# Hybrid decoder step on one core: where the state-space output is turned, activated and split, and where the first GLU weights and x are loaded

## The chip, the cores and the metric

The kernel runs on one core of one Trainium2 chip. A core has TensorE (PE: matrix products and transposes), VectorE (DVE), ScalarE (ACT), GpSimd (POOL) and the engine that issues most DMA transfers, SyncE (SP). Each engine works through its own list in order and waits on semaphores. The metric is the time of one launch in microseconds (us), the median of several runs.

## The reference

One layer of a hybrid decoder for 256 prompt tokens and 8 samples of 8 tokens (320 columns in all), width 2048, all in f32:

```python
h = x * (1 + sc1) + sh1
q, k, v, u, ga, gb = split(h @ w_in)
att = stick_breaking(q, k_all, v_all)          # samples also read 1024 cached keys and values
y_s = s5(u, ssm_h0, ...)                       # state space branch, 1024 wide, plus d_skip * u
y_s = gelu(y_s)
y_s = y_s * sigmoid(y_s @ w_glu + b_glu)       # GLU, w_glu is 1024 x 1024
merged = sigmoid(ga) * (att @ w_att_br) + sigmoid(gb) * (y_s @ w_ssm_br)
x = layernorm(ALPHA * x + (1 + g1) * (merged @ w_out))
# then conv FFN, second layernorm
```

## The kernel before

Activations stand transposed: 128 features on the partitions, the 320 tokens in the free dimension, one such tile per block of 128 features (`KA` = 8 blocks for 1024 features, `KD` = 16 for 2048). Every f32 product is made of three products of rounded values: a value is split into a high part (`wH`, `ygH`, ... : rounded) and a low part (`wL`, `ygL`, ... : the rest), and `product` (L936 to L951) gives, for each of K blocks, high x high, high x low and low x high. For GLU and merge that is 8 blocks, 24 matmuls of 128x320 for each tile of the output. ACT makes the high part of a block of weights (L1251), DVE the low part (L1523), both one product ahead with two buffers, and SP loads weight blocks into a ring of four buffers (`load`, L440 to L443), each when the block four places before has been split. Semaphores `hi_done`, `split_done` and `chunk_done` count the blocks over the whole program in the order GLU (8), merge (32), out and so on.

The stages that matter here, in order of time:

1. Attention. `attend(i)` exists on every engine and is run for i = 0 to 8. It holds the front half for sample i (keys of 8 pages are loaded into `kpage`, transposed on PE as `flip`, copied by DVE and ACT, multiplied with the queries as `score`) and the back half for sample j = i - 1 together with prompt head j. The back half is a chain: `turn_scores` and `head_scores` on PE, `scores` and `head_scores` on DVE, `softplus` on ACT (Exp, then Ln) and DVE, `sums` on PE (with running sums over pages by POOL, `sR`), `log_weights` on DVE, `weights` on ACT (Exp), `outputs` on PE (values of 8 pages, L1117 to L1129), `copy_outputs` on ACT, `turn_outputs` on PE (L1142), `sample_output` on DVE. i = 1 to 7 are a loop; the last, `attend(SB, front=False)`, is written out and has a back half alone.
2. The state-space output. It was stored earlier by token in `y_tok`, and SP loads it back into `ytk` after attend(1) (L574, L575), with x behind it (L576, 2560 KB into `xT`, which had been spilled to `x_d`). After the last attend, PE transposes it (L1188: three transposes for each of 8 blocks), DVE adds the skip term (`ypre`, L1903), ACT applies the GELU (`ygl`, L1417), and DVE splits the result into `ygH` and `ygL` (L1907, L1908).
3. GLU. SP loads `w_glu` once all eight `ypre` are there (L579 waits for `y_pre`). There are eight products m = 0 to 7; after each, ACT takes the sigmoid (`gl_gate`, L1428), DVE multiplies and splits (L1921 to L1924), and both split the block of weights for product m + 2.
4. Merge: 32 products from 16 blocks each of `w_att_br` and `w_ssm_br`, and with each a gate of 160 KB that is loaded back (L591). x is needed only after it, by the residual of the out stage.

Of the kernel before, what the change touches and what calls it, by code (L numbers as in the profile page):

```python
# [5 lines left out]
P = 128  # L6
# [5 lines left out]
ds = bass.ds  # L12
# [72 lines left out]
def hybrid_step(nc, x_prompt, x_sample, cache_k, cache_v, state_ssm_re, state_ssm_im, state_conv, page_table,  # L85
# [52 lines left out]

    pring = [at(f"pring{i}", [P, KD, P], r_vtok + i * KD * P * 4) for i in range(2)]
# [78 lines left out]
    ypre = [at(f"ypre{i}", [P, T], r_vtok + i * CH) for i in range(2)]  # L218
    ygl = [at(f"ygl{i}", [P, T], r_vtok + (2 + i) * CH) for i in range(2)]
# [212 lines left out]
    with block:  # L432

        @block.sync
        def _(sp):
# [140 lines left out]
            sp.dma_start(xT[:].rearrange("p k t -> p (k t)"), x_d).then_inc(S["x_landed"], 16)  # L576
# [9 lines left out]
            with sp.Fori(0, KD // 2) as i:  # L586
# [271 lines left out]
        def _(pe):  # L858
# [78 lines left out]
            def product(n, cc, K, half_n, high, low, ready=None, first=0, end=None):  # L937
# [5 lines left out]
                a, b = wH[cc % 2], wL[cc % 2]  # L943
# [108 lines left out]
            def attend(i, front=True, back=True):  # L1052
# [92 lines left out]

                if front:
                    flip(0)
# [4 lines left out]
                if back:  # L1152
                    turn_scores()
                    head_scores()
                if front:
                    flip(2)
                    score(i, 0)
                    flip(3)
                    flip(4)
                    score(i, 1)  # L1160
                if back:
                    sums()
                if front:
                    flip(5)
                    flip(6)
                    score(i, 2)
                if back:
                    outputs()
                if front:
                    flip(7)  # L1170
                if back:
                    turn_outputs()

# [5 lines left out]

            pe.wait_ge(S["att_s"], SB + 1)  # L1180

            pe.wait_ge(S["ytk_landed"], 32)
            for c in range(KA):
                if c >= 4:
                    pe.wait_ge(S["y_pre"], c - 3)
                for tt in range(3):
                    rows = min(P, T - tt * P)
                    last = t.transpose(bank[4 + c % 4][:, tt * P:tt * P + rows], ytk[0:rows, tt, c * P:(c + 1) * P], ident[0:rows, 0:rows])  # L1188
                last.then_inc(S["ytk_turned"], 1)


            pe.wait_ge(S["y_ready"], KA)
            passes(pe, "glu", None, 0, lambda i, _: [products(i, GLU, cc, KA, ygH, ygL) for cc in range(4)])
# [32 lines left out]
        def _(act):  # L1226
# [123 lines left out]

            def attend(i, front=True, back=True):
# [26 lines left out]

                def copy_outputs():
# [33 lines left out]
            for c in range(KA):  # L1413
                act.wait_ge(S["y_pre"], c + 1)
                if c >= 2:
                    act.wait_ge(S["y_ready"], c - 1)
                a.activation(ygl[c % 2][:], ypre[c % 2][:], ACT.Gelu_apprx_tanh).then_inc(S["y_gelu"], 1)  # L1417


            start_stream(GLU, ks_of["glu"])  # L1420

            def glu_pass(i, next_ks):
                for cc in range(4):
                    wait_product(i, GLU, cc)
                    m = i * 4 + cc
                    if m >= 2:
                        act.wait_ge(S["s_ready"], m - 1)
                    a.activation(gl_gate[cc % 2][:], bank[cc % 2][:, 0:T], ACT.Sigmoid,  # L1428
                                 bias=par[:, P + 120 + m:P + 121 + m]).then_inc(acc_free[cc % 2], 1)
                    split_ahead(i, GLU, cc, next_ks, ks_of["glu"])  # L1430

            glu_pass(0, ks_of["glu"])
            glu_pass(1, ks_of["merge"])
# [51 lines left out]
        def _(dve):  # L1485
# [324 lines left out]

            def attend(i, front=True, back=True):
# [29 lines left out]

                def log_weights():
# [3 lines left out]
                    v.scalar_tensor_tensor(out=pe_[:], in0=masks[:], scalar=1e30, in1=pz[:], op0=MUL, op1=ADD).then_inc(S["p_arg"], 1)  # L1846
                    dve.wait_ge(S["s_cs"], j + 1)
# [36 lines left out]
                if back:  # L1884
                    head_output()
                if front:
                    read_page(7)
                if back:
# [10 lines left out]
            for c in range(KA):  # L1899
                dve.wait_ge(S["ytk_turned"], c + 1)  # L1900
                if c >= 2:
                    dve.wait_ge(S["y_gelu"], c - 1)
                v.scalar_tensor_tensor(out=ypre[c % 2][:], in0=projT[:, c, :], scalar=cw[:, 3 * 2 * JF + c:3 * 2 * JF + c + 1],  # L1903
                                       in1=bank[4 + c % 4][:, 0:T], op0=MUL, op1=ADD).then_inc(S["y_pre"], 1)
                if c >= 1:
                    dve.wait_ge(S["y_gelu"], c)
                    own.step(v.tensor_copy(ygH[:, c - 1, :], ygl[(c - 1) % 2][:]))  # L1907
                    v.tensor_tensor(ygL[:, c - 1, :], ygl[(c - 1) % 2][:], ygH[:, c - 1, :].bitcast(F32), SUB).then_inc(S["y_ready"], 1)  # L1908
            c = KA
            dve.wait_ge(S["y_gelu"], c)  # L1910
            own.step(v.tensor_copy(ygH[:, c - 1, :], ygl[(c - 1) % 2][:]))
            v.tensor_tensor(ygL[:, c - 1, :], ygl[(c - 1) % 2][:], ygH[:, c - 1, :].bitcast(F32), SUB).then_inc(S["y_ready"], 1)


            start_stream(GLU, ks_of["glu"])
            for m in range(KA):
# [8 lines left out]
                split_ahead(i, GLU, cc, ks_of["glu"] if i == 0 else ks_of["merge"], ks_of["glu"])  # L1925
# [160 lines left out]
```

## Time and profile before

| what | value |
|---|---|
| time, median of 3 runs | 2376.44 us (2372.89 to 2376.91) |
| time of the profiled execution | 2373.0 us, of which span 2371.2 us |
| mean granted TensorE clock | 0.952 of full |
| PE busy | 2183.9 us (92%) |
| DVE busy | 1203.3 us (51%) |
| ACT busy | 739.4 us (31%) |
| POOL busy | 340.0 us (14%) |
| attention, sample by sample (from the loads of its values to the next) | 25.0, 34.5, 28.0, 29.5, 29.6, 28.6, 27.9 us |
| last attend (back half alone) | 1021 to 1049 us |
| state-space output turned, activated, split | 1049 to 1060 us |
| GLU products | 1065 to 1098 us |
| merge products | from 1100.7 us |

PE is the busiest engine by far. Its idle time counts where the chain that ended last runs through another engine or a transfer. Times in the rows further down are counted from the start of the span.

### The profile page before, as it was taken

What the parts mean: (1) busy time and instruction counts of PE and PEld (TensorE: products, weight loads), DVE (VectorE), ACT (ScalarE), POOL (GpSimd) and SP (SyncE); (2) the same over time, 40 slices, a digit from 0 to 9 for tenths busy, and PEclk for the clock granted to TensorE, in tenths of its full rate; (3) what the DMA queues carried; (4) which work ended last, traced back from release to release, by engine and by line L of the source; (5) the groups of instructions that cost most, each with busy time, mean ns of one, the idle gap of its engine ahead of it and who ended that gap; (6) DMA issues with size and microseconds to landing.
All of it is one profiled execution on the core that took longest, in us unless ns stands there. A gap on an engine that the chain in (4) does not pass through costs nothing.

```text
span 2371.2 us, 41471 instructions
## 1 busy us (share of the span) xinstructions
PE 2183.9 (92%) x15407; PEld 1976.8 (83%) x15407; DVE 1203.3 (51%) x1786; ACT 739.4 (31%) x945; POOL 340.0 (14%) x632
## 2 busy tenths in 40 slices
PE   4869999999999888869999799999999999999996
PEld 2358788889999755539999689999999999999995
DVE  4743233323374344446654566644665456546665
ACT  1012222222222334433322354323333233233323
POOL 0104535300023301100000111000110001001002
PEclk8689999999899989979999979999999999999999
DMA  9899999996555897735676325446554655465441
GB/s 265 320 296 319 307 318 309 324 340 175 165 151 166 285 350 295 294 106 155 195 209 162 91 72 156 133 140 173 144 150 125 168 147 141 117 181 144 124 122 58
DMA packets 579059, 467.83 MB, mean 197 GB/s; under 512 B 17010, under 2 KB 503378, under 8 KB 578370
## 3 DMA queue, kind: packets, MB, share of 16 engines
q1 hardware_dynamic: 568971, 439.30, 61.1%
q0 software_dynamic: 6720, 19.64, 2.4%
q10 hardware_dynamic: 3264, 7.44, 0.9%
q8 instruction: 72, 1.18, 0.2%
q14 instruction: 32, 0.26, 0.0%
HBM read 440.13 MB, written 26.21 MB: 197 GB/s over the span
## 4 chain that ended last, share of the span: by engine, by line
PE 57%; DVE 4%; issue 2%; ACT 1%; DMA 1%; SPq 1%; POOL 1%; POOLq 0%; DVEq 0%; ACTq 0%
PE bank L947 16%; PE bank L949 16%; PE bank L948 16%; PE bank L1061 2%; PE bank L1126 1%; PE bank L1076 1%; PE bank L1206 1%; PE bank L1202 1%; DMA kpage<-in_cache_k 1%; POOL xT L816 1%; PE bank L1107 0%; PE bank L1110 0%; DVE hL L1999 0%; DVE res L1994 0%; ACT wH L1251 0%
## 5 line engine op out<-in xcount | busy, mean ns | idle before, releaser
L947 PE MATMUL bank<-hH,wH 128*128 128x320 f32 x2432 | 767.3, 316 | 25.1 <-DVE hL L1999 17.3
L948 PE MATMUL bank<-hL,wH 128*128 128x320 f32 x2432 | 758.1, 312 | 0.0
L949 PE MATMUL bank<-hH,wL 128*128 128x320 f32 x2432 | 757.8, 312 | 0.0
L1523 DVE TENSOR_TENSOR wL<-ring,wH 128x2048 fp32r<-128x2048 f32 (+3 forms) x208 | 391.3, 1881 | 268.3 <-ACT wH L1251 268.3
L947 PEld LDWEIGHTS bank<-hH,wH 128*128 128x128 f32 x2432 | 462.3, 190 | 67.7 <-issue 48.1
L948 PEld LDWEIGHTS bank<-hL,wH 128*128 128x128 f32 x2432 | 463.0, 190 | 0.0
L949 PEld LDWEIGHTS bank<-hH,wL 128*128 128x128 f32 x2432 | 462.6, 190 | 0.0
L1251 ACT ACTIVATE wH<-ring 128x2048 fp32r<-128x2048 f32 (+3 forms) x208 | 330.1, 1587 | 381.6 <-PE bank L949 376.2
L1528 DVE TENSOR_TENSOR wL<-pring,wH 128x2048 fp32r<-128x2048 f32 x64 | 177.1, 2769 | 369.3 <-ACT wH L1256 368.7
L947 PE MATMUL bank<-fH,wH 128*128 128x320 f32 x704 | 218.7, 311 | 11.2 <-DVE fL L2032 11.2
L948 PE MATMUL bank<-fL,wH 128*128 128x320 f32 x704 | 218.2, 310 | 0.0
L949 PE MATMUL bank<-fH,wL 128*128 128x320 f32 x704 | 218.1, 310 | 0.0
L898 PE MATMUL bank<-ring,c_cols 128*32 128x512 f32 x768 | 116.3, 708 | 42.6 <-DMA ring<-in_w_ada 42.5
L947 PEld LDWEIGHTS bank<-fH,wH 128*128 128x128 f32 x704 | 132.7, 189 | 12.3 <-DVE fL L2032 12.3
L948 PEld LDWEIGHTS bank<-fL,wH 128*128 128x128 f32 x704 | 132.7, 189 | 0.0
L949 PEld LDWEIGHTS bank<-fH,wL 128*128 128x128 f32 x704 | 132.7, 189 | 0.0
L840 POOL COPY rows_out<-ext 128x2 f32 x88 | 16.8, 190 | 783.0 <-ACT ext L1467 783.0
L1256 ACT ACTIVATE wH<-pring 128x2048 fp32r<-128x2048 f32 x64 | 121.9, 1904 | 13.6 <-DMA pring<-in_w_in 13.6
L1467 ACT ACTIVATE ext<-bank 128x256 f32<-128x256 f32 x88 | 34.0, 386 | 225.2 <-PE bank L949 222.2
L898 PEld LDWEIGHTS bank<-ring,c_cols 128*32 128x32 f32 x768 | 19.0, 117 | 96.7 <-DMA ring<-in_w_ada 70.9
L816 POOL TENSOR_TENSOR xT<-xT,rstd 128x320 f32<-128x320 f32 x32 | 27.0, 883 | 418.9 <-DVE rstd L1984 418.9
L1335 ACT ACTIVATE gate<-bank 128x320 f32<-128x320 f32 x32 | 14.0, 437 | 215.0 <-PE bank L949 215.0
(383 smaller groups left out, 2872.6 us busy)
## 6 DMA issues: line engine op xcount, KB each, us to landing
ring<-in_w_ada SPq DMA_DIRECT2D x96, 1024.0 KB, 11.0
ring<-in_w_up SPq DMA_DIRECT2D x88, 1024.0 KB, 5.8
pring<-in_w_in SPq DMA_DIRECT2D x64, 1024.0 KB, 8.2
kpage<-in_cache_k SPq DMA_DIRECT2D x64, 512.0 KB, 5.9
vpage<-in_cache_v SPq DMA_DIRECT2D x64, 512.0 KB, 5.7
ring<-in_w_down SPq DMA_DIRECT2D x32, 768.0 KB, 5.0
ring<-in_w_down SPq DMA_DIRECT2D x32, 640.0 KB, 4.5
ring<-in_w_out SPq DMA_DIRECT2D x16, 1024.0 KB, 6.0
```

Of the source, the lines that this page charges most:

```text
L816: g.tensor_tensor(xT[:, k, :], xT[:, k, :], rstd[:], ALU.mult).then_inc(S["scaled"], 1)
L898: last = t.matmul(bank[2][k * QUAD:(k + 1) * QUAD, :], c_cols[:, unit * UNITS + k, :], wide(ring[s])[:, k, :], start=(unit == 0), stop=(un ...
L947: t.matmul(acc, a[:, k, :], high[:, k, :], start=(k == 0), stop=False)
L948: t.matmul(acc, a[:, k, :], low[:, k, :], start=False, stop=False)
L949: last = t.matmul(acc, b[:, k, :], high[:, k, :], start=False, stop=(k == K - 1))
L1061: last = t.transpose(bank[flip_banks[p % 2][h // 4]][:, (h % 4) * P:(h % 4 + 1) * P], kpage[p][:, h * HD:(h + 1) * HD], ident[:])
L1076: last = t.matmul(bank[7][quad * QUAD:(quad + 1) * QUAD, m * PAGE:(m + 1) * PAGE], q_flat[:, f * 4 * (QUAD + ST) + hh * QUAD:f * 4 * (QUAD ...
L1251: a.activation(wH[cc % 2][:, 0:K, :], ring[cc][:, 0:K, :], ACT.Copy).then_inc(S["hi_done"], 1)
L1256: a.activation(wH[e][:], pring[e][:], ACT.Copy).then_inc(S["hi_done"], 1)
L1467: a.activation(ext[cc][:, 2:2 + NP], b[:, 0:NP], ACT.Copy).then_inc(S["conv_ev"], 1)
L1523: v.tensor_tensor(wL[cc % 2][:, 0:K, :], ring[cc][:, 0:K, :], wH[cc % 2][:, 0:K, :].bitcast(F32), SUB)\
L1528: v.tensor_tensor(wL[e][:], pring[e][:], wH[e][:].bitcast(F32), SUB).then_inc(S["split_done"], 1)
```

## The change

The work of stages 2 and 3 up to the first product moves into the last attend, which is written out and has room where other samples flip keys.

On PE, blocks 0 to 3 of `ytk` are transposed behind `head_scores`, blocks 4 to 7 behind `sums` (into banks 0, 1, 2 and 6 in place of 4 to 7), and GLU product 0 stands between `outputs` and `turn_outputs`. On DVE the skip terms stand around `softplus`, the split of the first GLU weights within `log_weights`, and the splits of the activated blocks around `head_output`. On ACT the high parts of the first two blocks of GLU weights stand ahead of `softplus` and the eight GELUs ahead of `weights`; they work in place, with eight `ypre` buffers in the place of two `ypre` and two `ygl`. The GLU weights have buffers of their own (`gring`, four, where x's tile lies; `gH`, `gL`), so that four of their eight loads can be issued behind `ytk`, where x was loaded; the other four go out as these are split. x is loaded behind the loads of the first merge pass.

```diff
@@ SP
             sp.dma_start(ytk[0:SB * ST, 2, :], y_tok[NP:T]).then_inc(S["ytk_landed"], 16)
-            sp.dma_start(xT[:].rearrange("p k t -> p (k t)"), x_d).then_inc(S["x_landed"], 16)
+            for m in range(RING):
+                glu_weights(m)
             with sp.Fori(2, SB) as i:
                 attend(i)
             attend(SB, front=False)
-            sp.wait_ge(S["y_pre"], KA)
-            with sp.Fori(0, KA // 4) as i:
-                for cc in range(4):
-                    load(i * 4 + (GLU + cc), cc, KA, w_glu_d[:, :, ds((i * 4 + cc) * P, P)])
+            for m in range(RING, KA):
+                sp.wait_ge(S["split_done"], GLU + m + 1)
+                glu_weights(m)
+            sp.wait_ge(S["pv_rows"], SB + 1)
...
+            merge_loads(0)
+            sp.wait_ge(S["split_done"], RING + MERGE)
+            sp.dma_start(xT[:].rearrange("p k t -> p (k t)"), x_d).then_inc(S["x_landed"], 16)
+            with sp.Fori(1, KD // 2) as i:
+                merge_loads(i)
@@ PE, attend
+                def turn_y(c):
+                    if c == 0:
+                        pe.wait_ge(S["ytk_landed"], 32)
+                    if c >= 4:
+                        pe.wait_ge(S["y_pre"], c - 3)
+                    for tt in range(3):
+                        rows = min(P, T - tt * P)
+                        last = t.transpose(bank[y_banks[c % 4]][:, tt * P:tt * P + rows], ytk[0:rows, tt, c * P:(c + 1) * P], ident[0:rows, 0:rows])
+                    last.then_inc(S["ytk_turned"], 1)
...
                     turn_scores()
                     head_scores()
+                if not front:
+                    for c in range(4):
+                        turn_y(c)
...
+                if not front:
+                    for c in range(4, KA):
+                        turn_y(c)
                 if back:
                     outputs()
...
+                if not front:
+                    glu_product(0)
                 if back:
                     turn_outputs()
@@ ACT, attend
                 if back:
                     copy_scores()
+                if not front:
+                    for m in range(2):
+                        split_glu(m)
...
+                if not front:
+                    for c in range(KA):
+                        gelu(c)
                 if back:
                     weights()
@@ DVE, attend
+                else:
+                    for c in range(4):
+                        y_sum(c)
                 if back:
                     softplus()
...
+                else:
+                    for c in range(4, KA):
+                        y_sum(c)
                 if back:
                     log_weights()
...
+                else:
+                    for c in range(3):
+                        y_split(c)
                 if back:
                     head_output()
...
+                else:
+                    for c in range(3, KA):
+                        y_split(c)
+                    split_glu(1)
                 if back:
                     sample_output()
```

What stands on PE in the last attend from the last matmul of `sums` to `outputs` (bank3 takes the sums over the samples' pages, `vh` is the head's values). Before:

```order
L1110 MATMUL bank3<-sS_134,later_54 128x512
L1112 MATMUL bank3<-sR_135,ones_55 128x512
L1117 MATMUL bank4<-pe__137,vh_145 128x256
L1118 MATMUL bank4<-pe__137,vh_145 128x128
L1126 MATMUL bank5<-vpage0_114,se_133 32x512 x2
```

Now:

```order
L1128 MATMUL bank3<-sR_143,ones_55 128x512
L1169 MATMUL bank0<-ident_52,ytk_187 128x128 x2
L1169 MATMUL bank0<-ident_52,ytk_187 128x64
L1169 MATMUL bank1<-ident_52,ytk_187 128x128 x2
L1169 MATMUL bank1<-ident_52,ytk_187 128x64
L1169 MATMUL bank2<-ident_52,ytk_187 128x128 x2
L1169 MATMUL bank2<-ident_52,ytk_187 128x64
L1169 MATMUL bank6<-ident_52,ytk_187 128x128 x2
L1169 MATMUL bank6<-ident_52,ytk_187 128x64
L1133 MATMUL bank4<-pe__145,vh_153 128x256
L1134 MATMUL bank4<-pe__145,vh_153 128x128
```

The transposes of blocks 4 to 7 now stand behind the sums and ahead of the outputs.

What stands on DVE in the last attend from the end of `softplus` to the end of `log_weights` (`pe_` and `se` are the arguments that ACT raises to weights). Before:

```order
L1840 SCALAR_TENSOR_TENSOR pS_138<-masks_56,pS_138 128x384
L1845 TENSOR_TENSOR pz_136<-pz_136,bank4 128x384
L1846 SCALAR_TENSOR_TENSOR pe__137<-masks_56,pz_136 128x384
L1848 TENSOR_TENSOR se_133<-sz_132,bank3 128x512
L1849 TENSOR_TENSOR sz_132<-sz_132,bank4 8x64
L1850 SCALAR_TENSOR_TENSOR se_133<-mask_new_61,sz_132 8x64
```

Now:

```order
L1877 SCALAR_TENSOR_TENSOR pS_146<-masks_56,pS_146 128x384
L1881 SCALAR_TENSOR_TENSOR ypre4_192<-projT_83,cw_51,bank0 128x320
L1881 SCALAR_TENSOR_TENSOR ypre5_193<-projT_83,cw_51,bank1 128x320
L1881 SCALAR_TENSOR_TENSOR ypre6_194<-projT_83,cw_51,bank2 128x320
L1881 SCALAR_TENSOR_TENSOR ypre7_195<-projT_83,cw_51,bank6 128x320
L1892 TENSOR_TENSOR pz_144<-pz_144,bank4 128x384
L1893 SCALAR_TENSOR_TENSOR pe__145<-masks_56,pz_144 128x384
L1846 TENSOR_TENSOR gL0_79<-gring0_73,gH0_77 128x1024
L1897 TENSOR_TENSOR se_141<-sz_140,bank3 128x512
L1898 TENSOR_TENSOR sz_140<-sz_140,bank4 8x64
L1899 SCALAR_TENSOR_TENSOR se_141<-mask_new_61,sz_140 8x64
```

Four skip terms, which need the transposes that PE makes behind its sums, and one split of weights now stand within the chain that leads to the weights.

What SP issues from the last block of the first merge pass on, now (before, the load of `ring0` came right behind `gate3`):

```order
L447 DMA ring3_68<-in_w_ssm_br 128x8x128
L601 DMA gate3_206<-gates_d 128x320
L605 DMA xT_62<-x_d 128x5120
L606 UNCONDITIONAL_BRANCH
L606 ISA
L447 ISA
L447 DMA ring0_65<-in_w_att_br 128x8x128
```

x goes out ahead of the weights for merge product 4.

## Rows read from the trace of the kernel before

**Rows 1.** The chain that ended last, 1000 to 1130 us: start, length, engine, tile, line.

```profile
1046.92 0.60 ACT o_rows L1381
1047.66 1.05 PE bank L1142 x8
...
1057.91 0.55 DVE ypre L1903
1058.90 4.03 DMA ring<-in_w_glu
1062.95 1.06 ACT wH L1251
...
1065.32 0.64 PE bank L947
```

**Rows 2.** Timeline of the last attend: start, length; in brackets idle before, releaser.

```profile
1026.83 0.68 ACT L1367 ACTIVATE se<-se 128x576 f32<-128x576 f32 x1 [3.18 <-DVE se L1826]
...
1028.49 1.28 ACT L1370 ACT_TABLE_LOAD   x1
...
1035.37 0.55 DVE L1845 TENSOR_TENSOR pz<-pz,bank 128x384 f32<-128x384 f32 x1 [2.51 <-PE bank L1108]
1035.96 0.56 DVE L1846 SCALAR_TENSOR_TENSOR pe__137<-masks,pz 128x384 f32<-128x384 f32 x1
...
1036.83 1.02 PE L1112 MATMUL bank<-sR,ones 128*128 128x512 f32 x2
...
1037.89 0.69 DVE L1848 TENSOR_TENSOR se<-sz,bank 128x512 f32<-128x512 f32 x1 [1.38 <-PE bank L1112]
...
1038.98 0.68 ACT L1377 ACTIVATE se<-se 128x576 f32<-128x576 f32 x1 [1.91 <-DVE se L1850]
...
1039.81 0.78 PE L1117 MATMUL bank<-pe__137,vh 128*128 128x256 f32 x2 [1.95 <-ACT se L1377]
```

**Rows 3.** Timeline of the state-space output behind the last attend.

```profile
1049.28 6.67 PE L1188 MATMUL bank<-ident,ytk 128*128 128x128 f32 x24 [0.57 <-DVE attL L1864]
...
1049.95 1.12 DVE L1903 SCALAR_TENSOR_TENSOR ypre<-projT,cw,bank 128x320 f32<-128x320 f32 x2 [0.73 <-PE bank L1188]
...
1057.15 0.32 DVE L1907 CAST ygH<-ygl 128x320 fp32r<-128x320 f32 x1
```

**Rows 4.** Timeline of GLU products 1 (first and last matmul) and 2 (first).

```profile
1071.47 0.31 PE L947 MATMUL bank<-ygH,wH 128*128 128x320 f32 x1
...
1072.29 0.49 DVE L1921 TENSOR_TENSOR gl_part<-ygH,ygL 128x320 f32<-128x320 f32 x1 [4.52 <-ACT gl_gate L1428]
...
1074.11 1.22 DVE L1523 TENSOR_TENSOR wL<-ring,wH 128x1024 fp32r<-128x1024 f32 x1
...
1074.85 0.31 PE L949 MATMUL bank<-ygH,wL 128*128 128x320 f32 x1
...
1075.38 0.41 PE L947 MATMUL bank<-ygH,wH 128*128 128x320 f32 x1 [0.23 <-DVE wL L1523]
```

**Rows 5.** Stretches: PE, PEld, DVE, ACT, POOL busy (instructions), PEclk, DMA share, GB/s.

```profile
830.00:835.00 5.00, 4.62 (x21) 2.79 (x20) 2.77 (x6) 1.52 (x3) 0.16 (x1) 0.80 1.02 409
...
1037.00:1038.00 1.00, 0.85 (x2) 0.02 (x1) 0.11 (x1) 0.07 (x1) 0.00 (x0) 1.00 0.00 0
...
1065.00:1070.00 5.00, 4.68 (x17) 4.68 (x18) 1.49 (x2) 2.34 (x2) 0.00 (x0) 0.50 1.04 286
```

**Rows 6.** The chain that ended last, 820 to 900 us: the wait for a key page.

```profile
830.18 17.26 DMA kpage<-in_cache_k
```

**Rows 7.** DMA issues: size, median us from issue to landing.

```profile
ring<-in_w_glu SPq DMA_DIRECT2D x8, 512.0 KB, 4.8
...
xT<-x_d SPq DMA_DIRECT2D x1, 2560.0 KB, 17.6
```

**Rows 8.** Timelines of SP and of ACT around the start of merge.

```profile
1098.56 0.35 SPq L591 DMA_DIRECT2D gate<-gates_d  x1
...
1113.05 1.06 ACT L1251 ACTIVATE wH<-ring 128x1024 fp32r<-128x1024 f32 x1 [2.46 <-PE bank L949]
```

More of the change, by code:

```diff
@@ L137, in hybrid_step @@
     wL = [at(f"wL{i}", [P, KD, P], r_split + (2 * i + 1) * KD * P * 4, F32R) for i in range(2)]
+    gring = [at(f"gring{i}", [P, KA, P], r_x + i * 4096) for i in range(RING)]
+    gH = [at(f"gH{i}", [P, KA, P], r_split + i * 4096, F32R) for i in range(2)]
+    gL = [at(f"gL{i}", [P, KA, P], r_split + 8192 + i * 4096, F32R) for i in range(2)]
     pring = [at(f"pring{i}", [P, KD, P], r_vtok + i * KD * P * 4) for i in range(2)]
@@ L217, in hybrid_step @@
     ytk = at("ytk", [P, 3, SW], r_h + 5 * AW * 4)
-    ypre = [at(f"ypre{i}", [P, T], r_vtok + i * CH) for i in range(2)]
-    ygl = [at(f"ygl{i}", [P, T], r_vtok + (2 + i) * CH) for i in range(2)]
+    ypre = [at(f"ypre{i}", [P, T], r_vtok + i * CH) for i in range(KA)]
+    y_banks = (0, 1, 2, 6)
     ygH, ygL = at("ygH", [P, KA, T], r_q, F32R), at("ygL", [P, KA, T], r_k, F32R)
@@ L575, in _, with glu_weights @@
             sp.dma_start(ytk[0:SB * ST, 2, :], y_tok[NP:T]).then_inc(S["ytk_landed"], 16)
[L576 removed]
+            def glu_weights(m):
+                sp.dma_start(gring[m % RING][:], w_glu_d[:, :, m * P:(m + 1) * P]).then_inc(ring_landed[m % RING], 16)
+            for m in range(RING):
+                glu_weights(m)
             with sp.Fori(2, SB) as i:
@@ L579, in _, with merge_loads @@
             attend(SB, front=False)
-            sp.wait_ge(S["y_pre"], KA)
-            with sp.Fori(0, KA // 4) as i:
-                for cc in range(4):
-                    load(i * 4 + (GLU + cc), cc, KA, w_glu_d[:, :, ds((i * 4 + cc) * P, P)])
-            with sp.Fori(0, KD // 2) as i:
+            for m in range(RING, KA):
+                sp.wait_ge(S["split_done"], GLU + m + 1)
+                glu_weights(m)
+            sp.wait_ge(S["pv_rows"], SB + 1)
+            def merge_loads(i):
                 for cc in range(4):
@@ L935, in state_weights, with product @@
                 last.then_inc(S["w_flipped"], 1)
-            def product(n, cc, K, half_n, high, low, ready=None, first=0, end=None):
+            def product(n, cc, K, half_n, high, low, ready=None, first=0, end=None, weights=None):
                 if first == 0:
@@ L942, in product @@
                 acc = bank[cc % 2][:, 0:T]
-                a, b = wH[cc % 2], wL[cc % 2]
+                a, b = weights or (wH[cc % 2], wL[cc % 2])
                 for k in range(first, end or K):
@@ L1170, in attend, with glu_product @@
                     flip(7)
+                if not front:
+                    glu_product(0)
                 if back:
                     turn_outputs()
+            def glu_product(m):
+                if m == 0:
+                    pe.wait_ge(S["y_ready"], KA)
+                product(GLU + m, m, KA, nth_pair(GLU) + m // 2, ygH, ygL, weights=(gH[m % 2], gL[m % 2]))
             attend(0, back=False)
@@ L1177, in _ @@
             attend(SB, front=False)
+            for m in range(1, KA):
+                glu_product(m)
             pe.wait_ge(S["att_s"], SB + 1)
[L1182 to L1193, printed above, removed]
             pe.wait_ge(S["s_ready"], KA)
@@ L1349, in _, with split_glu @@
             act.wait_ge(S["flips_read"], 4 + 8 + KD + 5 + 18)
+            def split_glu(m):
+                act.wait_ge(ring_landed[m % RING], (nth_round(GLU) + m // RING) * 16 + 16)
+                act.wait_ge(S["chunk_done"], GLU + m + 1)
+                a.activation(gH[m % 2][:], gring[m % RING][:], ACT.Copy).then_inc(S["hi_done"], 1)
             def attend(i, front=True, back=True):
@@ L1377, in weights, with gelu @@
                     a.activation(se[:], se[:], ACT.Exp).then_inc(S["s_w"], 1)
+                def gelu(c):
+                    act.wait_ge(S["y_pre"], c + 1)
+                    a.activation(ypre[c][:], ypre[c][:], ACT.Gelu_apprx_tanh).then_inc(S["y_gelu"], 1)
                 def copy_outputs():
@@ L1410, in _ @@
             attend(SB, front=False)
[L1413 to L1433, printed above, removed]
+            for m in range(KA):
+                act.wait_ge(S["chunk_done"], GLU + m + 3)
+                if m >= 2:
+                    act.wait_ge(S["s_ready"], m - 1)
+                a.activation(gl_gate[m % 2][:], bank[m % 2][:, 0:T], ACT.Sigmoid,
+                             bias=par[:, P + 120 + m:P + 121 + m]).then_inc(acc_free[m % 2], 1)
+                if m + 2 < KA:
+                    split_glu(m + 2)
+                else:
+                    split_high(MERGE + m + 2 - KA, m + 2 - KA, KA, nth_round(MERGE))
             passes(act, "merge", None, 0, lambda i, ks: [split_ahead(i, MERGE, cc, ks, ks_of["merge"]) for cc in range(4)])
@@ L1809, in _, with split_glu @@
             new = sS[:, PAGES, :]
+            def split_glu(m):
+                dve.wait_ge(S["hi_done"], GLU + m + 1)
+                v.tensor_tensor(gL[m % 2][:], gring[m % RING][:], gH[m % 2][:].bitcast(F32), SUB).then_inc(S["split_done"], 1)
             def attend(i, front=True, back=True):
@@ L1840, in softplus, with y_sum, y_split @@
                     v.scalar_tensor_tensor(out=pS[:], in0=masks[:], scalar=1.0, in1=pS[:], op0=ADD, op1=MUL).then_inc(S["p_s"], 1)
+                def y_sum(c):
+                    dve.wait_ge(S["ytk_turned"], c + 1)
+                    v.scalar_tensor_tensor(out=ypre[c][:], in0=projT[:, c, :], scalar=cw[:, 3 * 2 * JF + c:3 * 2 * JF + c + 1],
+                                           in1=bank[y_banks[c % 4]][:, 0:T], op0=MUL, op1=ADD).then_inc(S["y_pre"], 1)
+                def y_split(c):
+                    dve.wait_ge(S["y_gelu"], c + 1)
+                    own.step(v.tensor_copy(ygH[:, c, :], ypre[c][:]))
+                    v.tensor_tensor(ygL[:, c, :], ypre[c][:], ygH[:, c, :].bitcast(F32), SUB).then_inc(S["y_ready"], 1)
                 def log_weights():
@@ L1846, in log_weights @@
                     v.scalar_tensor_tensor(out=pe_[:], in0=masks[:], scalar=1e30, in1=pz[:], op0=MUL, op1=ADD).then_inc(S["p_arg"], 1)
+                    if not front:
+                        split_glu(0)
                     dve.wait_ge(S["s_cs"], j + 1)
@@ L1887, in attend @@
                     read_page(7)
+                else:
+                    for c in range(3, KA):
+                        y_split(c)
+                    split_glu(1)
                 if back:
@@ L1896, in _ @@
             attend(SB, front=False)
[L1899 to L1915, printed above, removed]
             for m in range(KA):
@@ L1924, in _ @@
                 v.tensor_tensor(sL[:, m, :], gl_part[:], sH[:, m, :].bitcast(F32), SUB).then_inc(S["s_ready"], 1)
-                split_ahead(i, GLU, cc, ks_of["glu"] if i == 0 else ks_of["merge"], ks_of["glu"])
+                if m + 2 < KA:
+                    split_glu(m + 2)
+                else:
+                    split_low(MERGE + m + 2 - KA, m + 2 - KA, KA)
             def merge_pass(i, next_ks):
```

## The prediction, made before the changed kernel ran

> **What bounds the kernel now.** PE is busy for 92% of the span, so only stretches in which the chain that ended last leaves PE, or in which PE runs at its low clock, can give time. I read that chain first, around the end of attention. It runs through PE's outputs, the copy on ACT, the turned outputs on PE, then through the skip terms on DVE, a transfer of GLU weights, their split on ACT and DVE, and only at 1065.32 into GLU product 0 [rows 1]. Between 1048.7 and 1065.3 PE does 6.7 us of transposes and nothing else [rows 1, 3]. The stretches show a second loss: product 0 starts at the granted clock 0.50, which is 1.2 of 2.4 GHz, 17 matmuls in 4.68 busy us [rows 5], where those of product 1 start (1074.85 - 1071.47) / 23 = 0.147 us apart [rows 4]. The third view is the timeline of the last attend, into which the work goes: its back half is a chain across engines with PE waiting [rows 2].
>
> Gain and loss are read at one point on both sides: the start of GLU product 2, 1075.38 before [rows 4]. From there on the pattern of one product, one sigmoid, one DVE group and one split ahead is the same in both kernels. All times are on the clock of before.
>
> **The change part by part.**
>
> *Transposes 0 to 3, skip terms 0 to 3, high parts of two weight blocks: nothing.* ACT has 3.18 us without work ahead of its first Exp [rows 2]; two copies of 1.06 [rows 1] fit. PE and DVE wait in that time for ACT's Exp, table load of 1.28 and Ln, so that DVE's four terms of 0.56 (1.12 for two) [rows 3] fit as well. The bound if the cover failed is those 2.2 us.
>
> *Transposes 4 to 7 and skip terms 4 to 7: +5.3 us on the attention's chain.* This is the part that costs. The lists of both engines show that PE makes these transposes behind the last matmul of the sums, which ends at 1036.83 + 1.02 = 1037.85 [rows 2], and DVE has the four terms ahead of `log_weights`. Before, DVE did the first two operations of `log_weights` at 1035.37 and 1035.96, while PE was still summing, and the third from 1037.89 [rows 2]. Now both sets queue behind the skip terms. Step by step: the first transposed block reaches DVE 0.67 us after PE starts (1049.28 to 1049.95), then one each 0.58 at the high clock, the last taking 0.54: 1037.85 + 0.67 + 3 x 0.58 + 0.54 = 1040.8. `pz` and `pe_` take 1.15 (0.55, 0.56 and the gaps), the low part of the first weights 1.22 [rows 4], the rest of `log_weights` 1.05 (1037.89 to 1038.94): 1044.2. ACT has the GELU of the last block by 1041.3, the table load for Exp by 1042.6 and the head's Exp by 1043.1, so it waits for DVE, with 1.1 us to spare. Its last Exp of 0.68 ends at 1044.95 and PE starts its outputs at 1045.1, against 1039.81 [rows 2]: 5.3 us later. At the low clock the transposes would come 0.9 apart (24 took 6.67, the first at the high clock) [rows 3] and the outputs start 1.2 later still, 6.5 in all. I take the high clock, which PE has at 1037 [rows 5], and keep 6.5 as the bound. If the sums, warmed by transposes 0 to 3, ran at the high clock too, 1 us would come back (estimate: half of the last two, 1.02 and the one ahead of it).
>
> *Outputs: unchanged, 7.1 us* (1039.81 to 1046.92 [rows 1, 2]), to 1052.2. They hide the splits of the activated blocks: one is 0.76 (cast at 1057.15, next term at 1057.91 [rows 1, 3]). Eight of them, 6.1, and the head's output on DVE, 0.9, end at 1044.2 + 7.0 = 1051.2, 1 us before PE asks. The second low part of weights ends at 1052.4, long before product 1.
>
> *GLU product 0 ahead of the turned outputs: starts at 1052.2 instead of 1065.32.* PE comes warm out of the outputs, so 24 x 0.147 = 3.5 us, to 1055.8. The turned outputs take 1.05 [rows 1], to 1056.8. The copy on ACT that they need is hidden behind product 0.
>
> *Product 1* runs from 1056.9 to 1060.4. Behind the turned outputs DVE has the sample's output (0.5, estimate from its two operations on 64 columns), the four operations of product 0's gate (1072.29 to 1074.11, 1.82) and the split for product 2 (1.22) [rows 4]: 1056.8 + 3.6 = 1060.4. Product 2 starts at about 1060.5, as DVE and PE finish together. **1075.38 - 1060.5 = 14.9 us gained.** The wait for GLU weights (4.03), their first split on ACT and DVE, and the low clock of product 0 (17 matmuls and a few more, at 4.68 / 17 - 0.147 = 0.13 each some 2.6 us) are inside this sum.
>
> *Four GLU loads in x's place behind `ytk`: +0.9 us.* In sample 2 the chain waits 17.26 us for a key page queued behind `ytk` and x [rows 6], at a DMA share of 1.02 and 409 GB/s [rows 5]. x is 2.62 MB, 6.4 us at that rate. The GLU blocks are 2.10 MB in 512-byte runs; such loads moved 286 GB/s at a share of 1.04 [rows 5], 7.3 us. Bounds: 1.3 gained, if only bytes count, to 1.5 lost. The Trainium skill (DMA: Bandwidth & Descriptors, Specifications) gives 512 B as the least transfer for line rate; by that the four would take 5.1 us and the term be a gain of 1.3, while the row shows a full share at 286 GB/s, so the trace disagrees and decides.
>
> *x behind the first merge loads: nothing.* It goes out behind `gate3` at 1098.56 [rows 8]. At 409 GB/s it passes by 1106; the load of merge block 4 queues behind it and needs 4.8 more [rows 7], about 1111. ACT asks for that block at 1113.05 [rows 8], 2 us later. Cover gone costs what is above those 2 us. x itself is needed a whole stage later.
>
> **Sum:** -14.9 + 0.9 = -14.0 us, or 2373.0 to 2359.0 for the profiled execution, whose span is 1.8 us shorter than its time. That execution lies 3.4 under the median of the three runs, which becomes 2376.4 - 14.0 = **2362.4**.
>
> **The rivals.**
>
> *A, as worked out*, 11.5 to 16 us faster, with the clock and DMA bounds above: 77%.
>
> *B, x is not hidden.* For: x took 17.6 us from issue to landing when others shared the DMA engines [rows 7]. From 1099 it would land at 1116.6, merge block 4 at 1118.5 or so, and ACT and PE stand for 5.5 us. Against: at that place little else moves, and at sample 2 the values of a whole sample stood in the queue ahead. Gain 8.5, 2367.9: 10%.
>
> *C, the clock falls in the longer gap ahead of the outputs and stays low through outputs and product 0.* PE waits some 4.5 us there in place of 1.95 [rows 2]. Product 0 would cost 3.1 more (24 x 0.13), the outputs up to 2.6 (an estimate: they took 7.1 with part of them at either rate). Gain 8.3, 2368.1: 7%. The Trainium skill (TensorE: Matmul & The Clock Gate, Part 1) says the count of matmuls at the low rate differs from run to run for one kernel; no row of before tests that, and it would widen A rather than shift it.
>
> *D, the GLU loads hold up sample 2.* If each of the four took its 4.8 from issue to landing one behind the other, they would need 19.2 instead of 6.4, and 12.8 go onto the key page. Gain 2, within the measurement: 4%. Against it, such loads moved 286 GB/s together [rows 5], and four at that rate are 7.3.
>
> *E, slower: PE keeps the low clock through GLU.* Each product then costs 3.1 more, and from 5 of 8 products on the gain of 14 is used up; with all eight it is 10.8 us slower, 2387. For: PE started GLU at 0.50 before [rows 5]. Against: it had stood for 9 us then, and was high again by product 1 [rows 4]; now it comes out of 7 us of outputs. 2%.
>
> **How the numbers follow.** Likeliest A, 2362.4. B and C lie near 2368 and hold 17%; D and E are left out, as is the fast end of A. Range 2356 to 2368.5. A measurement of this kernel can tell about 0.2%, 4.8 us. A, B and C are faster by more: 0.94. D is the same: 0.04. E is slower: 0.02.
>
> **What the changed profile would show.** The outputs start 5 to 7 us after where they did, counted from the last matmul of the sums, behind a DVE wait for transposes; no wait of PE between outputs, product 0, turned outputs and product 1; granted clock near 1 in product 0; no transfer in the chain between attention and GLU; the key page of sample 2 lands within 1.5 us of its old distance; merge block 4 has landed when ACT asks. Wrong would be: a PE wait for `ygH`/`ygL` ahead of product 0 (my slack is 1 us), one for GLU weights, one early in merge for `ring`, or a longer wait in sample 2.

## The result, and the profile of the changed kernel

The change makes the kernel faster by about 14 us. The median of seven runs is 2361.6 us (2358.33 to 2366.86), beside 2376.7 (2372.89 to 2381.08) for the kernel before on the same chip: a ratio of 0.9942, 95% interval 0.9931 to 0.9954, which is 10.9 to 16.4 us. The predicted time was 2362.4, in a range of 2356 to 2368.5. The profiled execution took 2364.43 us, with a span of 2362.8.

Its span is only 8.4 us shorter. Cutting both traces at three events shows where this comes from: the load of the first sample's new values (where attention starts on SP), the end of the last matmul of the sums in the last attend, and the start of GLU product 2. Before, the four stretches last 817.00, 220.85, 37.53 and 1295.82 us; after, 822.43, 220.23, 23.26 and 1296.88. The change touches the middle two, which are 14.9 us shorter; the first is 5.4 longer and the last 1.1. The first stretch has the same code in all kernels here, and over their profiled executions it lasts from 815.7 to 825.5 (815.7 in e7 and 824.2 in e6 below, which do the same up to there). So from here on everything is counted from an event, not from the span's start.

First the chain of the changed kernel that ended last, from the end of the sums on (start, length, engine, tile, line; it answers to [rows 1]):

```profile
1041.45 1.21 PE bank L1128 x2
1042.66 2.15 PE bank L1169 x12
1044.83 0.55 DVE ypre L1881
1045.38 0.47 DVE pz L1892
1045.88 0.56 DVE pe__145 L1893
1046.44 1.13 DVE gL L1846
1047.57 0.60 DVE se L1897
...
1048.57 0.69 ACT se L1411
1049.40 1.19 PE bank L1133 x2
...
1051.02 5.89 PE bank L1142 x32
1056.91 0.98 PE bank L1145 x4
...
1061.60 0.80 PE bank L1158 x8
1066.04 0.54 ACT gl_gate L1461
```

The transfer of GLU weights and the copy ahead of the turned outputs, both in [rows 1], are gone from it. What has come in between the sums and the outputs are transposes, a skip term, the first two operations of `log_weights` (`pz` and `pe_`) and one split of weights. The timeline of the same stretch (start, length; in brackets the idle time before and its releaser) answers to [rows 2 to 4]:

```profile
1027.95 1.99 ACT L1383 ACTIVATE gH<-gring 128x1024 fp32r<-128x1024 f32 x2
1031.23 0.68 ACT L1401 ACTIVATE se<-se 128x576 f32<-128x576 f32 x1 [1.29 <-DVE se L1863]
...
1043.12 2.26 DVE L1881 SCALAR_TENSOR_TENSOR ypre<-projT,cw,bank 128x320 f32<-128x320 f32 x4 [5.85 <-PE bank L1169]
...
1049.40 1.19 PE L1133 MATMUL bank<-pe__145,vh 128*128 128x256 f32 x2 [4.61 <-ACT se L1411]
...
1055.25 0.49 DVE L1887 TENSOR_TENSOR ygL<-ypre,ygH 128x320 fp32r<-128x320 f32 x1
...
1057.82 0.42 PE L963 MATMUL bank<-ygH,gH 128*128 128x320 f32 x1
...
1061.44 0.96 PE L1158 MATMUL bank<-o_sel,o_rows 128*128 128x16 f32 x8
1062.25 0.39 PE L963 MATMUL bank<-ygH,gH 128*128 128x320 f32 x1
...
1065.92 0.41 PE L963 MATMUL bank<-ygH,gH 128*128 128x320 f32 x1
```

PE waits 4.61 us for the last Exp where it waited 1.95, and from 1049.40 on it never waits: outputs, product 0, turned outputs and product 1 follow each other. ACT's two copies of weights fit into its idle time, which falls from 3.18 to 1.29. The stretches show the granted clock (columns as in [rows 5]):

```profile
1043.00:1048.00 5.00, 1.79 (x10) 1.01 (x9) 4.77 (x8) 3.69 (x6) 0.00 (x0) 1.00 0.00 0
...
1052.00:1053.00 1.00, 1.00 (x12) 0.20 (x5) 0.93 (x4) 0.00 (x0) 0.00 (x0) 0.50 0.00 0
1056.00:1057.00 1.00, 1.00 (x14) 0.14 (x5) 0.88 (x1) 0.00 (x0) 0.00 (x0) 1.00 0.00 0
1058.00:1059.00 1.00, 1.00 (x8) 1.00 (x9) 0.00 (x0) 0.98 (x2) 0.00 (x0) 1.00 0.57 154
...
1091.60:1095.60 4.00, 3.96 (x27) 3.97 (x28) 0.70 (x1) 0.15 (x1) 0.00 (x0) 1.00 0.85 364
```

The clock is 1.00 while DVE does the skip terms, 0.50 in most of the outputs, and 1.00 again before product 0 starts. The last row is the start of merge. Before, the same place ran at 0.62, 18 matmuls in 4 us against 27 now; why is open:

```profile
1100.70:1104.70 4.00, 4.00 (x18) 4.00 (x19) 0.75 (x1) 0.00 (x0) 0.00 (x0) 0.62 0.43 127
```

At sample 2, the chain of the changed kernel answers to [rows 6]. The 17.26 us of one key page's transfer have become four issues on SP, 12.80 us in all, and a short transfer:

```profile
834.17 0.58 SPq L582
834.79 5.40 SPq L582
840.24 4.93 SPq L582
845.21 1.76 SPq L582
...
848.00 5.62 DMA kpage<-in_cache_k
```

Last, the DMA issues (size, median us to landing) and the timelines of SP and ACT in merge, to [rows 7, 8]:

```profile
gring<-in_w_glu SPq DMA_DIRECT2D x8, 512.0 KB, 5.7
...
xT<-x_d SPq DMA_DIRECT2D x1, 2560.0 KB, 10.2
```

```profile
1089.65 0.42 SPq L605 DMA_DIRECT2D xT<-x_d  x1
1090.50 0.41 SPq L447 DMA_DIRECT2D ring<-in_w_att_br  x1
...
1098.97 1.06 ACT L1280 ACTIVATE wH<-ring 128x1024 fp32r<-128x1024 f32 x1 [2.46 <-PE bank L965]
1102.49 1.06 ACT L1280 ACTIVATE wH<-ring 128x1024 fp32r<-128x1024 f32 x1 [2.46 <-PE bank L965]
```

x lands at about 1099.9. Merge block 4 is asked for at 1102.49, and ACT's idle time before it is the usual 2.46, ended by PE and not by a DMA. x is hidden.

### The profile page after: what moved, and what is told of

Its sections match the earlier page's. It is cut to its first block, busy times and chain, and to the rows that moved or that the text cites. A ratio compares the mean times of both kernels' runs of the same rounds, so it can differ in the third digit from the quotient of the medians.

```text
span 2362.8 us, 41397 instructions
## 1 busy us (share of the span) xinstructions
PE 2188.5 (93%) x15407; PEld 1980.2 (84%) x15407; DVE 1201.4 (51%) x1786; ACT 738.9 (31%) x945; POOL 340.7 (14%) x632
## 4 chain that ended last, share of the span: by engine, by line
PE 57%; DVE 3%; issue 1%; ACT 1%; SPq 1%; POOL 1%; DMA 0%; POOLq 0%; DVEq 0%; ACTq 0%
PE bank L963 16%; PE bank L964 16%; PE bank L965 16%; PE bank L1077 2%; PE bank L1092 1%; PE bank L1142 1%; PE bank L1235 1%; PE bank L1231 1%; SPq L582 1%; POOL xT L832 1%; PE bank L1123 0%; PE bank L1126 0%; DVE hL L2047 0%; DVE res L2042 0%; SPq L554 0%
## 5 line engine op out<-in xcount | busy, mean ns | idle before, releaser
L963 PE MATMUL bank<-hH,wH 128*128 128x320 f32 x2432 | 767.9, 316 | 25.3 <-DVE hL L2047 17.3
L1556 DVE TENSOR_TENSOR wL<-ring,wH 128x2048 fp32r<-128x2048 f32 (+3 forms) x200 | 381.7, 1908 | 262.4 <-ACT wH L1280 262.4
L1280 ACT ACTIVATE wH<-ring 128x2048 fp32r<-128x2048 f32 (+3 forms) x200 | 321.5, 1608 | 377.6 <-PE bank L965 377.6
L1854 DVE COPY kTp<-bank 128x512 f32<-128x512 f32 x64 | 44.2, 690 | 73.9 <-PE bank L1077 36.9
```

The lines of the kernel that those rows point to most:

```text
L1280: a.activation(wH[cc % 2][:, 0:K, :], ring[cc][:, 0:K, :], ACT.Copy).then_inc(S["hi_done"], 1)
L1556: v.tensor_tensor(wL[cc % 2][:, 0:K, :], ring[cc][:, 0:K, :], wH[cc % 2][:, 0:K, :].bitcast(F32), SUB)\
L1854: v.tensor_copy(kTp[p % 2][:, 0:4, :].rearrange("p h k -> p (h k)"), bank[2 * (p % 2)][:]).then_inc(S["kt_dve"], 1)
```

## The experiments

One theory and two rivals were at stake. The theory: the gain is the closed gap between attention and GLU, less what transposes 4 to 7 and their skip terms add behind the sums. Rival one: ACT, with table loads, GELUs and splits, sets the outputs' start. Rival two: early weights and the place of x bring the gain. All runs stand in one table. Columns 2 and 3 are the middle stretches defined above, column 4 the wait from the end of the sums to the outputs, and column 5 the outputs' length to the end of the matmuls on `vnew`, all from one profiled execution. Times are medians with their range; the ratio is to the kernel before on the same chip (medians 2374.27 to 2377.85).

| kernel | attention to end of sums | to product 2 | to outputs | outputs | time, us | ratio (95%) |
|---|---|---|---|---|---|---|
| before | 220.85 | 37.53 | 1.96 | 7.07 | 2376.7 | 1 |
| after | 220.23 | 23.26 | 6.74 | 8.49 | 2361.6 | 0.9942 (0.9931-0.9954) |
| after, again | 221.76 | 23.08 | 6.75 | 8.29 | 2367.4 (2359.53-2375.38) | 0.9961 (0.9946-0.9976) |
| e1 | 220.67 | 17.06 | 1.95 | 7.08 | 2354.95 (2352.99-2357.87) | 0.9908 (0.9890-0.9926) |
| e3 | 220.00 | 32.48 | 1.95 | 7.12 | 2371.4 (2368.07-2375.7) | 0.9984 (0.9972-0.9995) |
| e4 | 211.64 | 21.44 | 5.78 | 6.92 | 2351.87 (2349.83-2357.24) | 0.9901 (0.9881-0.9920) |
| e5 | 213.32 | 37.44 | 1.95 | 7.07 | 2366.45 (2360.16-2374.88) | 0.9958 (0.9944-0.9972) |
| e6 | 213.77 | 23.08 | 6.74 | 8.30 | 2356.62 (2353.23-2363.62) | 0.9914 (0.9892-0.9936) |
| e7 | 214.56 | 17.10 | 1.95 | 7.11 | 2350.03 (2345.19-2352.5) | 0.9889 (0.9871-0.9907) |
| e8 | 212.94 | 17.30 | 1.95 | 7.12 | 2348.31 (2344.64-2354.37) | 0.9884 (0.9864-0.9905) |
| e9 | 213.45 | 18.25 | 1.95 | 7.11 | 2347.6 (2341.24-2351.09) | 0.9879 (0.9855-0.9902) |
| e10 | 213.93 | 17.30 | 1.95 | 7.08 | 2346.62 (2340.18-2351.01) | 0.9869 (0.9847-0.9891) |

What columns 2 and 3 lose against before agrees in most runs with what the time loses by the ratio: 14.9 for after (13.8), 20.7 for e1 (21.8), 25.3 for e4 (23.5), 7.6 for e5 (10.0), 28.1 for e8 (27.6), each inside the ratio's interval. The repeat of after is the exception: 13.5 by its profile and 9.3 (5.7 to 12.8) by the ratio. The rest of the program lies between 1295.8 and 1303.4 us without a pattern by edit.

### e1: all transposes ahead of the sums

```diff
                 if not front:
-                    for c in range(4):
+                    for c in range(KA):
                         turn_y(c)
...
-                if not front:
-                    for c in range(4, KA):
-                        turn_y(c)
                 if back:
                     outputs()
```

> The changed kernel with one edit: PE transposes blocks 4 to 7 behind blocks 0 to 3, ahead of its sums, and nothing else. Theory (the place of these transposes holds up log_weights and with it the outputs): the outputs start about 2 us after the last matmul of the sums instead of 6.9, the outputs take near 7.1 us again instead of 8.5 because the gap ahead of them is short, and the kernel is 5 to 6 us faster than the changed one, about 2356. Rival (ACT is what holds them up: eight GELUs and a table load stand ahead of its weights): the outputs still start 4 us or more later and the time stays near 2361.

Measured: the outputs start 1.95 us behind the sums, as before the change. The timeline of e1, in order of time:

```profile
1032.66 3.13 PE L1169 MATMUL bank<-ident,ytk 128*128 128x128 f32 x12 [0.55 <-DVE ypre L1878]
...
1037.02 1.91 DVE L1878 SCALAR_TENSOR_TENSOR ypre<-projT,cw,bank 128x320 f32<-128x320 f32 x4
...
1043.74 1.08 PE L1133 MATMUL bank<-pe__145,vh 128*128 128x256 f32 x2 [1.95 <-ACT se L1408]
```

Transposes 4 to 7 now run where PE waits for DVE's `pS`, and the skip terms where PE makes the sums. ACT still has both copies of weights, all eight GELUs and the same table loads ahead of its last Exp, so rival one falls: the 4.8 us were the place of this work on PE and DVE. The outputs take 7.08 us again. Together that is 6.2 us in the stretch to product 2, and the median of 2354.95 is what was expected.

### e3: early weights and late x, state-space output as before

Edit: `turn_y`, the skip terms and the GELUs go back behind the last sample, with product 0 behind them; the four early GLU loads, their two splits and x's new place stay.

> Half of the change: four GLU weight loads behind ytk, x behind the first merge loads, first high parts on ACT ahead of the GELUs; the transposes, skip terms, GELUs and splits stay behind the last attend, and their two low parts of weights behind them. Theory (the two halves are not additive, the y chain of 11 us is the larger one): from the last skip term to GLU product 0 some 3.4 us instead of 7.4, and 3 to 4 us faster than before, about 2373. Rival (the wait for the weights was the bulk): 8 us or more faster, 2368 or below.

Measured: 5.1 us in the stretch to product 2, 3.8 in time. The weights' part of the change, done alone, brings a fourth to a third of the whole, so rival two isn't the main cause.

### e4: state-space output inside, GLU loads only behind the skip terms

```diff
-            for m in range(RING):
-                glu_weights(m)
             with sp.Fori(2, SB) as i:
                 attend(i)
...
+            sp.wait_ge(S["y_pre"], KA)
+            for m in range(RING):
+                glu_weights(m)
```

ACT's first two splits go behind its last Exp, DVE's behind its splits of the activated blocks.

> The other half: the y work stands in the last attend as in the changed kernel, but SP loads the GLU weights only when all skip terms are there, and ACT and DVE split the first two blocks behind the Exp and behind the y splits; x behind the first merge loads as in the changed kernel. Theory (the early loads buy nothing, since the outputs hide a late load, and they cost in sample 2): PE still goes from outputs to product 0 with under 0.5 us of wait, the outputs start 1.2 us earlier as no weight split stands in log_weights, sample 2 is 3 to 5 us shorter, so 2356 to 2358. Rival (the early loads are what pays): PE waits 2 us or more for weights ahead of product 0, 2362 to 2366.

Measured: better than the whole change, 0.9901, and with 2351.87 faster than the theory's 2356 to 2358. SP issues the loads when the skip terms are done, and ACT waits little for the first (SP's, ACT's and PE's timelines; SP's row spans all eight issues, of which the first four end at 1034.57 and the others wait for their buffers):

```profile
1030.50 22.86 SPq L582 DMA_DIRECT2D gring<-in_w_glu  x8
...
1034.71 1.06 ACT L1384 ACTIVATE gH<-gring 128x1024 fp32r<-128x1024 f32 x1 [1.32 <-DMA gring<-in_w_glu]
...
1041.11 0.38 PE L964 MATMUL bank<-ygH,gH 128*128 128x320 f32 x1 [0.66 <-issue]
```

The outputs cover load and split but for 0.66 us of PE, a little above the 0.5 expected. Without the split of weights in `log_weights` they start 0.96 us earlier behind the sums than in after (5.78 against 6.74). Attention is 8.6 us shorter than in after, where 3 to 5 were expected. Run e5 tests what stands in x's old place.

### e5: the kernel before, x behind the first merge loads, nothing else

```diff
-            sp.dma_start(xT[:].rearrange("p k t -> p (k t)"), x_d).then_inc(S["x_landed"], 16)
             with sp.Fori(2, SB) as i:
...
+            merge_loads(0)
+            sp.dma_start(xT[:].rearrange("p k t -> p (k t)"), x_d).then_inc(S["x_landed"], 16)
+            with sp.Fori(1, KD // 2) as i:
+                merge_loads(i)
```

> The kernel before with x's load moved behind the loads of the first merge pass and nothing in its place. Theory (x in the queue behind ytk held up the key page of sample 2, on which PE stood 4.1 us; behind the first merge loads it is hidden): 3 to 4 us faster than before, about 2373, and no wait for a ring block in merge. Rival 1 (the DMA queue is full there anyway): sample 2 as long as before, 2376. Rival 2 (x is not hidden in merge): PE waits there for block 4, and the gain is lost.

Measured: 10 us (6.6 to 13.3), 7.5 of them in attention, where 3 to 4 were expected. The attention interval from the first to the last load of new values is 195.6 against 203.1; e4 and e6 to e10 give 194.2 to 196.4, after, its repeat, e1 and e3 201.9 to 204.1. The kernels of the first group have no bulk load between `ytk` and sample 2. In the second it is x in one and four GLU blocks in the others, at the same price. The stretches over the first two samples, of before and of e8:

```profile
817.00:876.55 59.55, 48.41 (x487) 32.10 (x486) 24.86 (x48) 22.23 (x35) 7.41 (x23) 0.86 0.98 378
```

```profile
816.74:869.14 52.40, 45.24 (x489) 29.64 (x488) 24.87 (x48) 22.32 (x35) 7.40 (x23) 0.93 1.00 381
```

The DMA engines are full in both (shares 0.98 and 1.00). Without the bulk load PE is idle for 7.2 us in place of 11.1, and needs 3.2 us less for the same matmuls, at a higher granted clock. That is how the cost shows on PE. Its size is near the load's own transfer time, an estimate: 2.62 MB of x at 378 GB/s are 6.9 us, and 2.10 MB of GLU blocks at the 286 GB/s of [rows 5] are 7.3. The two samples are shorter than before by 5.8 us in e5 (53.74) and 7.2 in e8. So it reads as if DMA bound them while a bulk load stood there, and each load added its own time, which would also explain the same price for both.

### e6, e7, e8: the places combined

e6 is the changed kernel with its four early GLU loads ahead of sample 7:

```diff
+            with sp.Fori(2, SB - 1) as i:
+                attend(i)
             for m in range(RING):
                 glu_weights(m)
-            with sp.Fori(2, SB) as i:
-                attend(i)
+            attend(SB - 1)
```

e7 is e6 with e1's edit, and e8 is e4 with e1's edit.

> The changed kernel, with SP's four early GLU weight loads ahead of attend(7) instead of behind ytk; nothing else moves. Theory (what stands in x's place costs 7 us there, because the queue is full behind ytk and the values of a sample, and would cost less in a later sample, where the DMA share is 0.79): first to last values load of attention 195 to 199 us instead of 202, the kernel 3 to 7 us faster than the changed one, 2355 to 2358. Rival (the cost belongs to the loads and goes where they go): 2361, with a wait of some 7 us for a key page in sample 7.

> e1 and e6 together: transposes 4 to 7 ahead of the sums, early weight loads ahead of attend(7). Theory (two independent costs): the gains of both add, 6 to 7 from the transposes and 3 to 7 from the loads, 2348 to 2352. Rival (they overlap): no better than the better one, 2355.

> e1 and e4 together: transposes 4 to 7 ahead of the sums, and all GLU weight loads only when the skip terms are there, which is now some 6 us earlier. Theory: the late loads still land under the outputs, attention takes 194 to 196 us from first to last values load, the outputs start about 2 us behind the sums, and the kernel is 28 us or more faster than before, 2344 to 2349, the fastest of all. Rival (with the outputs so early, DVE's splits of y and of the weights become the bound): PE waits 2 us or more ahead of product 0, and it is no faster than e4 by more than 2 us.

Measured: e6 takes 6.5 us off attention and leaves the rest alone. Its sample 7 takes 28.41 us with the four loads in it, at a DMA share of 0.96; before, it took 28.57 without them, at 0.79. The loads find room there, and the rival falls. The median of 2356.62 is as expected, though the changed kernel took 2367.4 on the same chip, so the difference between the two is more than the 3 to 7 us forecast. e7 and e8 have both gains, and their times lie where the theories had them. The chain of e8 shows what is left between sums and GLU:

```profile
1028.48 1.22 PE bank L1129 x2
1029.72 0.69 DVE se L1893
...
1030.81 0.69 ACT se L1409
1031.63 0.67 PE bank L1134 x2
...
1037.77 0.98 PE bank L1146 x4
...
1038.90 0.38 PE bank L964
```

Even with loads issued at 1026.16, behind the last skip term, product 0 finds its weights. So the early loads, once the state-space output is inside, buy nothing: e8 equals e7 within the intervals. Whether e8 is faster than e4 the intervals don't settle either (0.9884 and 0.9901); its middle stretches are 2.8 us shorter.

### e9, e10: two variants of e8

e9 puts product 0 behind the turned outputs; e10 issues the two loads of `ytk` ahead of sample 7.

> e8 with one edit: GLU product 0 stands behind the turned outputs on PE instead of ahead of them, so all eight products follow them. Theory (the place of product 0 only hides ACT's copy of the outputs and DVE's last output): PE waits 0.7 to 0.8 us for the copy behind the outputs, product 1 starts at most 1 us later than in e8 counted from the end of the sums, 14.0 to 14.6 against 13.6; time within 2 us of e8, 2347 to 2351. Rival (product 0's place is what keeps the clock up): product 0 runs at 0.50 of the clock and costs 3 us more.

> e8 with the loads of ytk moved from behind attend(1) to ahead of attend(7). Theory (what costs 7.5 us behind attend(1) is the backlog of a queue that is full there; without x the 1.25 MB of ytk fit): attention from first to last values load 193 to 195 us as in e8 (194.8), the same time within 2 us. Rival (any transfer in that place costs its own time): 3 us off samples 1 and 2 and the same on none, 191 to 192, time 2345.

Measured: in e9 PE waits where product 0 had stood in front:

```profile
1039.21 1.04 PE L1159 MATMUL bank<-o_sel,o_rows 128*128 128x16 f32 x8 [0.79 <-ACT o_rows L1415]
1040.09 0.39 PE L964 MATMUL bank<-ygH,gH 128*128 128x320 f32 x1
```

That is 0.95 us in the stretch to product 2, product 1 starts 14.33 us behind the sums as expected, and product 0 still runs at 1.00. The time shows no difference. So the order of product 0 and turned outputs is a small part of the change, below 1 us here. e10 doesn't shorten attention, 196.2 us against 194.8: `ytk`, 1.3 MB in its old place, costs nothing visible, and its rival falls. The first two samples of e10:

```profile
822.37:876.67 54.30, 47.52 (x484) 30.65 (x483) 24.64 (x48) 21.76 (x34) 7.41 (x23) 0.87 0.90 345
```

The DMA share is 0.90 here, and the samples are no shorter than the 52.40 of e8. A transfer costs its own time there only as long as DMA is the bound; what bounds the two samples then is open.

### after, again

> The changed kernel once more beside the next three, for comparison on one chip: 0.993 to 0.995 of the kernel before, about 2361. Sample 2 again with SP standing at its four weight loads for some 12 us.

Measured: 0.9961 (0.9946 to 0.9976), a median of 2367.4, so less gain than expected. SP stood at the four loads for 13.16 us. Both intervals overlap; the gain is 6 to 16 us by the two together, and the profiled middle stretches agree within 1.4 us. The difference lies outside them, and its cause is open.

## Why the prediction was right, point by point

The gap ahead of GLU closed as forecast, and the work behind the sums cost what was forecast. That the sum came within 1 us has luck in it: the outputs took 1.4 us more than forecast, while the outputs' start cost 0.5 less and attention up to the sums, where the GLU loads were priced at 0.9 lost, came out 0.6 shorter.

**Hidden parts: right.** ACT's two copies lie in its idle time. In both kernels the first matmul of the sums starts 9.91 us after the copy to `z_rows`, so transposes and skip terms 0 to 3 cost nothing. The 1 us that warmer sums might have given back did not come: they took 5.29 us, 4.89 before.

**Skip terms 4 to 7: +5.3 predicted, +4.8 measured** (6.74 - 1.96), at the high clock, which was the choice. e1 shows that place as the cause, not ACT, and by e4 0.96 of it is the split of weights. The sign "5 to 7 us after" was missed by 0.2.

**Outputs: unchanged was wrong by 1.4.** They took 8.49, not 7.1. The granted clock falls within the outputs before the change too, but for a shorter part of them (columns as in [rows 5]; before, then after):

```profile
1039.81:1046.88 7.07, 7.07 (x40) 2.09 (x40) 0.85 (x2) 0.00 (x0) 0.00 (x0) 0.76 0.00 0
```

```profile
1049.40:1057.89 8.49, 8.49 (x41) 2.66 (x41) 6.98 (x17) 0.00 (x0) 0.00 (x0) 0.63 0.16 46
```

This is the first half of rival C. Its second half, a slow product 0, did not come: its matmuls are 0.147 apart. All runs in which the outputs start 1.95 behind the sums have outputs of 7.07 to 7.12; the three with 6.7, of which PE is idle for 4.6, have 8.3 to 8.5. e4, with 5.78 and PE idle for 3.64, has 6.92, at a mean clock of 0.77, so a longer wait doesn't always cost; what decides is open. The Trainium skill (TensorE: Matmul & The Clock Gate, Part 1) says that for one kernel the count of matmuls at the low rate differs from run to run; the outputs of the changed kernel, 8.49 and 8.29 us in its two profiles, don't contradict it.

**From product 0 to product 2: right within 0.6 us.** Counted from the end of the sums, product 0 came at 15.16 (predicted 14.35), product 1 at 19.59 (19.05), product 2 at 23.26 (22.65). DVE had the last activated split at 1055.74, 2.1 us ahead of need. The gain here is 14.3; 14.9 was the sum. The earlier start of the outputs (0.5) took back part of what their length cost (1.4).

**GLU loads in x's place: +0.9 predicted, 0.8 at the key page, nothing in attention as a whole.** From the load of new values to the key page's landing 31.2 us now (853.62 - 822.43), 30.4 before; over all of attention 202.1, 204.1, 203.3 and 201.9 against 203.1. So exchanging the loads was near neutral. As a reading of the row the term missed the larger number: whatever stands there costs 7.5 us, and the prediction weighed only one load against the other.

**x in merge: right, rival B excluded.** Transfer and cover are as forecast. The higher clock at the start of merge, worth some 1.5 us there, wasn't forecast; it doesn't show in the last stretch (1295.82 and 1296.88), whose spread is larger.

**Rivals D and E excluded:** the key page is 0.8 us later, not 12.8, and PEclk is 1.00 in product 0 and in merge.

## What to carry to other kernels

Work that is moved into a chain across engines should go ahead of the step in which the chain's engine is busy, not behind it: the same transposes and skip terms, with one split of weights, cost 4.8 us behind the sums and nothing when the transposes stood ahead of them (e1). A bulk load is priced by taking it away, not by exchanging it for another: in samples where the DMA engines were already full it cost 7.5 us, half of what the whole change gained, and in sample 7, where their share had been 0.79, the same four blocks cost nothing. Once the state-space output stood in the last attend, prefetching GLU weights early bought nothing, as the outputs hide all but 0.2 to 0.7 us of a load issued just before them (e8, e4). The best versions, e7 to e10, lie at 0.987 to 0.989; which of them is fastest the intervals don't tell.

## What the hardware showed that was not expected

Issuing a DMA on SP itself took time when others stood before it: the four GLU issues held SP for 12.80 us (834.17 to 846.97), the last three for 5.40, 4.93 and 1.76, where x's single issue took 0.58 before. In e4, with a DMA share of 0.00 just before, the same four held SP for only 4.07 us (0.40, 0.58, 1.40 and 1.55), and ahead of sample 7 in e6 for 7.30. That the commands behind them would wait as long in the queue as on SP is argued from the neutral exchange, not shown by itself.

TensorE's granted clock falls to 0.50 within the outputs in every kernel here, and rises again. In the kernels whose outputs start 1.95 us behind the sums its mean over the outputs is 0.76; in the three executions in which PE stood idle for 4.6 us ahead of them it is 0.63 to 0.65, which cost 1.2 to 1.4 us. e4, with 3.64 us of idle time, has 0.77 and lost nothing.
